# Mixture-of-experts gates in a hybrid decoder layer: the one-hot products as two rounded products, with the scaling moved from VectorE to ScalarE and GpSimd

## What is computed

```python
q = (hf @ wq).reshape(T, PEER_HEADS, 2, PEER_HALF)
s = jnp.einsum('thcd,hcnd->thcn', q, subkeys)
sv, si = lax.top_k(s, PEER_TOPK)
...
fv, fpos = lax.top_k(cand.reshape(...), PEER_TOPK)
gates = jax.nn.softmax(fv, axis=-1)
...
u = jnp.take(U, ic, axis=0)
act = jax.nn.gelu(jnp.einsum('chkd,cd->chk', u, xc), approximate=False)
vv = jnp.take(V, ic, axis=0)
return jnp.einsum('chk,chkd->cd', gc * act, vv)
```

## Time and profile before

| What | us |
|---|---|
| median of 3 runs | 1926.75 (1925.65 to 1927.59) |
| the profiled execution, its own time | 1926.39 |
| its span | 1924.7 |
| TensorE busy | 1830.3 (95%) |
| VectorE busy | 1452.9 (75%) |
| ScalarE busy | 732.0 (38%) |
| GpSimd busy | 588.2 (31%) |
| L1963, the products of the one-hot matrices, busy | 67.3 + 33.7 |
| L2190 and L2195, making them, busy | 43.8 + 21.9 and 71.1 + 35.5 |

### The profile page before, as it was taken

How to read it: one execution, slowest core, us unless ns; L and a number is a source line. 1 busy time by engine, 2 the same in 40 slices (tenths; PEclk the granted TensorE clock), 3 DMA queues, 4 the chain that set the end, 5 groups by cost and what they waited for, 6 DMA issues and landing times.

```text
span 1924.7 us, 32918 instructions
## 1 busy us (share of the span) xinstructions
PE 1830.3 (95%) x10454; PEld 1619.1 (84%) x10454; DVE 1452.9 (75%) x2936; ACT 732.0 (38%) x1316; POOL 588.2 (31%) x446
## 2 busy tenths in 40 slices
PE   3999799999889999999999999999999999999996
PEld 3677688886379999999999999999988888888885
DVE  6786556664838787849888898867688888888887
ACT  2342334451244545553333333333333333333331
POOL 5013522230043534453232332345233233333310
PEclk8999899999989999999999999999999999999998
DMA  8741000004523333358889988899899999999981
GB/s 309 257 145 33 1 1 1 1 1 149 204 82 118 132 116 123 129 190 276 296 298 311 308 291 288 292 333 386 345 400 385 356 348 357 355 356 354 352 292 70
DMA packets 245051, 435.06 MB, mean 226 GB/s; under 512 B 84898, under 2 KB 157956, under 8 KB 244996
## 3 DMA queue, kind: packets, MB, share of 16 engines
q1 hardware_dynamic: 208132, 300.12, 45.1%
q0 software_dynamic: 36864, 134.23, 18.8%
HBM read 379.77 MB, written 54.53 MB: 226 GB/s over the span
## 4 chain that ended last, share of the span: by engine, by line
PE 70%; DVE 1%; ACT 0%; issue 0%; ACTq 0%; DVEq 0%
PE bank L1573 28%; PE bank L1980 9%; PE bank L1982 9%; PE bank L1981 9%; PE bank L1553 6%; PE bank L1917 5%; PE bank L1963 4%; PE bank L1929 1%; DVE n_stats L1329 0%; DVE wide L2293 0%; DVE wide L2291 0%; DVE wide L1338 0%; PE bank L1922 0%; DVE wide L1343 0%; ACT uh L1581 0%
## 5 line engine op out<-in xcount | busy, mean ns | idle before, releaser
L1573 PE MATMUL bank<-hh,uh 128*128 128x384 f32 x1024 | 357.1, 349 | 0.0
L1573 PE MATMUL bank<-hl,uh 128*128 128x384 f32 x1024 | 343.0, 335 | 0.0
L1980 PE MATMUL bank<-vh,wh 128*128 128x512 f32 x768 | 299.5, 390 | 3.1 <-DVE wl L2252 3.1
L1981 PE MATMUL bank<-vl,wh 128*128 128x512 f32 x768 | 299.5, 390 | 0.0
L1982 PE MATMUL bank<-vh,wl 128*128 128x512 f32 x768 | 299.4, 390 | 0.0
L1631 POOL DMA_INDIRECT vsel<-in_peer_v,picks x128 | 152.2, 1189 | 413.0 <-DVE gt L1657 398.4
L2085 ACT ACTIVATE vh<-vraw 128x1024 fp32r<-128x1024 f32 x128 | 135.9, 1062 | 286.5 <-PE bank L1982 269.0
L1631 POOL DMA_INDIRECT wide<-in_peer_u,picks x108 | 148.0, 1370 | 232.8 <-DVE wide L1638 218.6
L2249 DVE TENSOR_TENSOR vl<-vraw,vh 128x1024 fp32r<-128x1024 f32 x128 | 156.6, 1224 | 80.8 <-ACT vh L2085 80.0
L1573 PE MATMUL bank<-hh,ul 128*128 128x384 f32 x1024 | 198.9, 335 | 0.0
L1573 PEld LDWEIGHTS bank<-hl,uh 128*128 128x128 f32 x1024 | 192.9, 188 | 0.0
(11 more groups left out here) (341 smaller groups left out, 3207.9 us busy)
## 6 DMA issues: line engine op xcount, KB each, us to landing
urows<-in_peer_u SPq DMA_DIRECT2D x128, 512.0 KB, 6.1
vraw<-in_peer_v SPq DMA_DIRECT2D x128, 512.0 KB
scored<-act_out SPq DMA_DIRECT2D x128, 192.0 KB
gates<-SS SPq DMA_DIRECT2D x16, 1536.0 KB
gtile<-gates SPq DMA_DIRECT2D x32, 768.0 KB
act_in<-scored SPq DMA_DIRECT2D x128, 192.0 KB
wt<-in_w_in SPq DMA_DIRECT2D x19, 512.0 KB
wq<-in_peer_wq SPq DMA_DIRECT2D x18, 512.0 KB, 3.8
```

The source lines that it names most:

```text
L1573: last = pe.matmul(bank, u[:, k, :], h[:, k, 0:TD], start=(n == 0), stop=(n == 3 * KD - 1))
L1980: pe.matmul(b, wh[s][:, cols], vh[s][:, half], start=first, stop=False)
L1981: pe.matmul(b, wh[s][:, cols], vl[s][:, half], start=False, stop=False)
```

## The change

The share of a pick is split in a rounded part `gate_hi` and the remainder `gate_lo`. VectorE now makes two plain one-hot matrices for a step, `OI` and `OJ`, with one comparison each. ScalarE multiplies `OJ` by the rounded share into `OH` (`high`, four ACTIVATEs, one per token, the share as a pointer operand for the scale), GpSimd multiplies it by the remainder into `OL` (`low`, one instruction for the four tokens). TensorE multiplies `OI` by `OH` and by `OL`, both products in the rounded form, adding the second onto the first. Slots are two instead of three, so `hot_step` waits for step n - 2, and TensorE waits for `hot_hi`, `hot_lo` and the copy of step n - 2. GpSimd's fetches keep their waits, but are placed between the multiplies of a block. `OI`, `OH`, `OL` and the split shares lie in buffers of the routing (`wqh`, `wql`), which is over by then.

```diff
-        SLOTS = 3
+        SLOTS = 2
-        OI = [SS[:, 3, 0:4, :], SS[:, 3, 4:8, :], st2[:, 4:8, :]]
-        OJ = [SS[:, 7, 0:4, :], SS[:, 7, 4:8, :], q2[0][:, :].rearrange("p (t n) -> p t n", t=4)]
+        OI, OH, OL = ([four(m, q) for q in range(SLOTS)] for m in (wqh[0], wqh[1], wql[0]))
+        OJ = [SS[:, 3, 0:4, :], SS[:, 3, 4:8, :]]
+        gate_hi, gate_lo = shares_of[:, 0:TD], shares_of[:, 512:512 + TD]
...
# GpSimd
+            def low(i, q):
+                n = STEPS * i + q
+                pool.wait_ge(hot, START + n + 1)
+                pool.tensor_tensor(OL[q % SLOTS], OJ[q % SLOTS],
+                                   gate_lo[:, 4 * n:4 * n + 4].bitcast(F32).unsqueeze(2).broadcast_to([P, 4, P]),
+                                   ALU.mult).then_inc(hot_lo, 1)
             pool.wait_ge(picks_up, START + 1)
+            fetched(0, 3, 0, 3)
+            pool.wait_ge(glo_up, START + 1)
             for i in range(BLOCKS):
-                fetched(0, 3, 3 * i, 3)
+                for s in range(4):
+                    for q in steps_of(s):
+                        low(i, q)
+                    if i == BLOCKS - 1:
+                        continue
+                    if s == 1:
+                        for k in range(3):
+                            row_u(k, 3 * (i + 1) + k, 3)
+                    elif s == 2:
+                        row_v(0, 3 * (i + 1), 3)
+                    elif s == 3:
+                        row_v(1, 3 * (i + 1) + 1, 3)
+                        row_v(2, 3 * (i + 1) + 2, 3)
...
# TensorE
             pe.wait_ge(t_out, START + 3)
+            pe.wait_ge(ghi_up, START + 1)
...
-                        pe.wait_ge(hot, START + n + 1)
-                        pe.wait_ge(staged, START + n - 2)
+                        pe.wait_ge(hot_hi, START + n + 1)
+                        pe.wait_ge(hot_lo, START + n + 1)
+                        pe.wait_ge(staged, START + n - 1)
                         for k in range(4):
-                            last = pe.matmul(banks[4 + q % SLOTS][:, k * P:(k + 1) * P], OI[q % SLOTS][:, k, :],
-                                             OJ[q % SLOTS][:, k, :], start=True, stop=True)
+                            at = banks[4 + q % SLOTS][:, k * P:(k + 1) * P]
+                            pe.matmul(at, OI[q % SLOTS][:, k, :], OH[q % SLOTS][:, k, :], start=True, stop=False)
+                            last = pe.matmul(at, OI[q % SLOTS][:, k, :], OL[q % SLOTS][:, k, :], start=False, stop=True)
...
# ScalarE
+            act.activation(gate_hi, banks[6][:, 0:TD], ACT.Copy).then_inc(ghi_up, 1)
+            def high(b, o, q):
+                n = 2 * STEPS * b + (STEPS * o + q)
+                act.wait_ge(hot, START + n + 1)
+                for k in range(4):
+                    last = act.activation(OH[q % SLOTS][:, k, :], OJ[q % SLOTS][:, k, :], ACT.Copy,
+                                          scale=gate_hi[:, bass.ds(4 * n + k, 1)].bitcast(F32))
+                last.then_inc(hot_hi, 1)
...
                             sel.gelus(act, 0, 3, 3 * (i - SPREAD))
+                        for q in steps_of(s):
+                            high(b, o, q)
                         for q in steps_of(s):
                             act.wait_ge(spread, ...)
...
# VectorE
+            dve.tensor_tensor(gate_lo, turned[2][:, :], gate_hi.bitcast(F32), ALU.subtract).then_inc(glo_up, 1)
             def hot_step(i, q):
-                dve.wait_ge(spread, START + n - 2)
-                dve.tensor_tensor(OI[q % SLOTS], iota..., turned[0]..., ALU.is_equal)
-                for k in range(4):
-                    at = bass.ds(4 * n + k, 1)
-                    last = dve.tensor_scalar(OJ[q % SLOTS][:, k, :], iota[:, :], turned[1][:, at], turned[2][:, at],
-                                             ALU.is_equal, ALU.mult)
+                dve.wait_ge(spread, START + n - 1)
+                for m, key in ((OI, turned[0]), (OJ, turned[1])):
+                    last = dve.tensor_tensor(m[q % SLOTS], iota..., key[:, bass.ds(4 * n, 4)]..., ALU.is_equal)
                 last.then_inc(hot, 1)
```

More of the change, by code:

```diff
@@ L1724, in emit_experts, with four @@
                                                       (act_out[:, :, :], "p s t -> p (s t)")))
-        SLOTS = 3
+        SLOTS = 2
         turned = [m.rearrange("p u n -> p (u n)") for m in (last3[:, 0:3, :], last3[:, 4:7, :], st2[:, 0:3, :])]
-        OI = [SS[:, 3, 0:4, :], SS[:, 3, 4:8, :], st2[:, 4:8, :]]
-        OJ = [SS[:, 7, 0:4, :], SS[:, 7, 4:8, :], q2[0][:, :].rearrange("p (t n) -> p t n", t=4)]
+        def four(m, q):
+            return m[:, 4 * q:4 * q + 4, :]
+        OI, OH, OL = ([four(m, q) for q in range(SLOTS)] for m in (wqh[0], wqh[1], wql[0]))
+        OJ = [SS[:, 3, 0:4, :], SS[:, 3, 4:8, :]]
+        shares_of = wql[1][:, :, :].rearrange("p k n -> p (k n)")
+        gate_hi, gate_lo = shares_of[:, 0:TD], shares_of[:, 512:512 + TD]
         stage = [SS[:, 4 * b:4 * b + 3, :, :].rearrange("p h t n -> p (h t n)")
@@ L1743, in emit_experts @@
         hot, spread, staged = sem("hot"), sem("spread"), sem("staged")
+        hot_hi, hot_lo, ghi_up, glo_up = sem("hot_hi"), sem("hot_lo"), sem("ghi_up"), sem("glo_up")
         sent = [sem(f"sent{b}") for b in range(2)]
@@ L1874, in _, with row_u, row_v @@
             scores.remainder(pool, SPREAD, 0)
+            def row_u(k, at, back):
+                if at >= back:
+                    pool.wait_ge(sel.dot_up, START + at - back + 1)
+                sel.fetch(pool, sel.usel[k], sel.rows[0], at, sel.us_in[k])
+            def row_v(k, at, back):
+                if at >= back:
+                    pool.wait_ge(sel.y_up, START + 1 + at - back + 1)
+                sel.fetch(pool, sel.vsel[k], sel.rows[1], at, sel.vs_in[k])
             def fetched(first, c, done, back):
                 for k in range(c):
-                    if done + k >= back:
-                        pool.wait_ge(sel.dot_up, START + done + k - back + 1)
-                    sel.fetch(pool, sel.usel[first + k], sel.rows[0], done + k, sel.us_in[first + k])
+                    row_u(first + k, done + k, back)
                 for k in range(c):
-                    if done + k >= back:
-                        pool.wait_ge(sel.y_up, START + 1 + done + k - back + 1)
-                    sel.fetch(pool, sel.vsel[first + k], sel.rows[1], done + k, sel.vs_in[first + k])
+                    row_v(first + k, done + k, back)
+            def low(i, q):
[4 more added lines that the diff above has]
+                                   ALU.mult).then_inc(hot_lo, 1)
             pool.wait_ge(picks_up, START + 1)
+            fetched(0, 3, 0, 3)
+            pool.wait_ge(glo_up, START + 1)
             for i in range(BLOCKS):
-                fetched(0, 3, 3 * i, 3)
+                for s in range(4):
[11 more added lines that the diff above has]
+                        row_v(2, 3 * (i + 1) + 2, 3)
             pool.wait_ge(scores.ul_up, START + 4 * SPREAD + 1)
@@ L2185, in _ @@
             dve.wait_ge(t_out, START + 3)
+            dve.wait_ge(ghi_up, START + 1)
+            dve.tensor_tensor(gate_lo, turned[2][:, :], gate_hi.bitcast(F32), ALU.subtract).then_inc(glo_up, 1)
             def hot_step(i, q):
                 n = STEPS * (i - SPREAD) + q
-                dve.wait_ge(spread, START + n - 2)
-                dve.tensor_tensor(OI[q % SLOTS], iota[:, :].unsqueeze(1).broadcast_to([P, 4, P]),
-                                  turned[0][:, bass.ds(4 * n, 4)].unsqueeze(2)
-                                  .broadcast_to([P, 4, P]), ALU.is_equal)
-                for k in range(4):
-                    at = bass.ds(4 * n + k, 1)
-                    last = dve.tensor_scalar(OJ[q % SLOTS][:, k, :], iota[:, :], turned[1][:, at], turned[2][:, at],
-                                             ALU.is_equal, ALU.mult)
+                dve.wait_ge(spread, START + n - 1)
+                for m, key in ((OI, turned[0]), (OJ, turned[1])):
+                    last = dve.tensor_tensor(m[q % SLOTS], iota[:, :].unsqueeze(1).broadcast_to([P, 4, P]),
+                                             key[:, bass.ds(4 * n, 4)].unsqueeze(2).broadcast_to([P, 4, P]),
+                                             ALU.is_equal)
                 last.then_inc(hot, 1)
```

1 line of the change is left out of this document (added).

## The result

| | median us | lowest to highest, runs |
|---|---|---|
| before | 1926.35 | 1925.65 to 1927.59, 4 |
| with the change | 1948.66 | 1946.06 to 1954.33, 4 |

The ratio is 1.0119, with a 95% interval of 1.0096 to 1.0142: the change makes the kernel 1.2% slower. The profiled execution took 1948.91 us (span 1947.2), 22.5 more than that of before.

The account below looks back on a forecast made before the run. TensorE was taken as the bound, busy 50.00 of 50.00 us in the stretch. Terms 0 + 12.6 + 4.8 + 5.0 + 1.0 = 23.4 us on the profiled 1926.39 gave 1950 us, 1.2% slower; range 1932 to 1968.

Parts of the forecast that it names:

- The products, 0: TensorE's steps: eight rounded products cost 0.111 us each, like the float32 records before, so no change.
- Rival 1: Weight loads don't hold the rounded products: 0.067 us each gives 1916 us, chance 0.09; 0.081 gives 1927, chance 0.04.
- VectorE, 0: VectorE's comparisons in the steps: 40 us less work, worth 0 because TensorE does not wait for VectorE.
- ScalarE, +12.6: Scalings before the first step of tiles 0 and 2: TensorE 0.36 and 0.43 us late in 16 blocks, +12.6 us.
- GpSimd and blocking, +4.8: Step 0 of each block: VectorE and GpSimd hinder each other, 0.3 us beyond ScalarE's lateness, 16 times, +4.8 us.
- The start, +5.0: First step of all: GpSimd's first multiply waits for six fetches, delaying TensorE once by 5.0 us.
- the clock, +1.0: After TensorE's standstill of over 4 us at the start, a lower granted clock adds 1.0 us.
- Rival 2: The feeders are in time for steps 0 and 3, only the start's loss stays: 1932 us, chance 0.08.
- Rival 3: VectorE and GpSimd block each other throughout the blocks: 1964 us, up to 1993, chance 0.07.

Follow-up runs that it names:

- half_columns: Changed kernel with each of a step's eight products multiplying only 64 of its 128 columns, the other gate columns left out: 1949.29 us, 1.0122.
- no_shares: Kernel before, with one VectorE comparison for `OJ` instead of four compare-and-multiplies, the shares left out: 1925.35 us, 0.9997.
- low_first: Changed kernel with GpSimd's multiply of step 0 ahead of its last fetch of V: 1948.72 us, 1.0117.
- all_three: Changed kernel, three first-block V fetches behind the first multiplies, ScalarE's first scalings before roundings, GpSimd's step 0 multiply before its last V fetch: 1925.94 us, 1.0002.
- both_orders: Changed kernel with ScalarE's early scalings and GpSimd's early step 0 multiply, but all six fetches still before the first multiply: 1931.74 us, 1.0027.
- single: Kernel before, with VectorE writing rounded one-hot matrices, shares included, one rounded product per token, remainders left out: 1881.53 us, 0.9777.
- wide: `all_three` with both products of a token as one 256-column matmul with one weight load, ScalarE copying and VectorE adding the halves: 1919.02 us, 0.9957.
- early_scale: Changed kernel with ScalarE scaling the first step of tiles 0 and 2 before the next tile's roundings; 1941 expected if only tile 2's wait went: 1943.38 us, 1.0074.
- one_product: Changed kernel with the second product of each pair left out, the feeding by ScalarE and GpSimd kept: 1920.15 us, 0.9957.

## Why the prediction was right, and where its terms were off

The forecast was 1950 us, and 1948.7 came; the case was the likeliest one. By its own steps:

- **The products, 0.** They held. The float32 rows with 1 and 64 columns told the price of a rounded product before it existed, and `half_columns` shows that it is no matter of streaming. The step came out 0.04 us cheaper than priced, inside the bounds. Rival 1 fell with that: neither 0.067 nor 0.081 per product was seen. The Trainium skill (TensorE: Matmul & The Clock Gate, section LDWEIGHTS) gives a load as its columns divided by 1.2, 107 ns for 128, and the 0.111 agrees; the 0.11 of L1155 with 64 columns is twice what it gives, so the load's length may not be the whole reason. The 81 ns of its section Back-to-back issue gap appear in no row with 128 weight columns here.
- **VectorE, 0.** Worth nothing, as `no_shares` shows. The predicted 40 us less busy time came as 17.2: the comparisons shrank by 37 us (172.3 to 135.4), but GpSimd's multiplies lengthened the dot products of L1638 from 1218 to 1385 ns, 108 of them, by 18 us.
- **ScalarE, +12.6.** Right in kind and place, too low. The price taken from the pointer scale of a 128 x 512 copy was 1.08 for four; they take 1.29, inside the bounds of 0.72 and 1.52. That is 0.21 a step, 16 x 2 x 0.21 = 6.7 us. The signal, put at 0.2, took 0.05 in tile 2 and 0.13 in tile 0 of `low_first` (1051.53 against 1050.11 + 1.29 = 1051.40), where ScalarE alone is late; that gives part of it back. ScalarE's own share is then 0.46 in tile 0 (3.44 - 2.98, by `low_first`) and 0.48 in tile 2, 16 x 0.94 = 15.0 us.
- **GpSimd and blocking, +4.8.** The mechanism exists (2.25 us instead of 1.22, a fetch of 1.46), but the term was too large: GpSimd adds 0.08 us to ScalarE's lateness in a block, not 0.3, some 1.3 us in all, and `low_first`, which takes it away, gains nothing that can be seen. This error and the shortfall of the term above nearly cancel, so the sum is better than its terms; that part is luck. What the prediction didn't draw from its two figures, 1011.39 and 1011.24, is that either engine alone makes step 0 nearly as late; a remedy for one alone gets less than half.
- **The start, +5.0 and the clock, +1.0.** 4.1 + 0.5 and 1.5; the wait is ended by GpSimd's multiply behind six fetches, as said, and `all_three` against `both_orders` prices the place at 5.8.
- **Rival 2** is what `both_orders` is: predicted 1932, measured 1931.7, although by other means than quick scalings. **Rival 3** did not come: VectorE is less busy than before in the stretch, 38.52 of 50 us against 43.01.

## What to carry to other kernels

A product with 128 weight columns and no more than 128 moving ones costs 0.11 us whatever it streams, so count the pairs of load and product: replacing a float32 product (two pairs) by two rounded ones changes next to nothing, while the two forms with fewer pairs, `single` and `wide`, were quicker. When work moves off an engine that isn't the bound onto two others that feed the bound, look at where in their hand-written lists it stands; the same instructions cost 22 us in one order and nothing in another. And if two feeders are late together, mend both before judging either.

## What the runs showed of the hardware

- A pair of load and product with 128 weight columns takes 0.11 us: in float32, where a full product is two pairs, for 1, 64 and 128 moving columns, and in rounded form for 64 (`half_columns`) and 128. Rounded, with 256 moving columns it takes 0.12, with 384 0.174: twice the columns for nearly nothing is what `wide` lives on. With 64 weight columns 0.055 and 0.11 were both seen.
- An ACTIVATE of 128 x 128 with a pointer scale takes 0.42 us and the next starts 0.29 later, where a plain copy takes 0.27.
- A GpSimd multiply and a VectorE instruction with two inputs in SBUF exclude each other: 2.25 us instead of 1.22. The fetches that GpSimd issues took 1.46 us beside VectorE's two-input comparisons, where 0.94 was seen before. The Trainium skill (SBUF — State Buffer, section Who interferes with whom) tells of the first; for the second it infers the opposite, that such an instruction does not stall a fetch. No run here took the comparisons away from beside the fetches, and with the change a fetch at 1029.88 took 0.94 although a dot product ran beside it from 1029.96 on, so that cause is only argued.
- After TensorE's idle 3.96 us the granted clock was still 1.00 for the next microsecond, in which the eight products of step 0 ran, and then 0.51 for some 3.2 us (2.4 and 1.2 GHz are its levels). The 12 products of the scores behind it took 3.70 us instead of 2.19. The price is not the same each time: in `low_first`, after 3.93 us of the same wait, the clock was 0.50 from 862 to 868 us, with step 0 at 862.53.
- A reordering can move a wait to a later place. `early_scale` has one of 4.0 us behind the blocks, where TensorE waits for VectorE's `late_remainder`; its length is more than the 2.4 us that the median lies above 1941. Four other runs have one like it, of 1.8 to 5.0 us, for that instruction or for the DMA of the rows, `one_product` one of 1.0, and the change has none. What sets it off was not tried.
